# Hybrid decoder step: state updates in pairs, token rows at both ends, a split first unit and shorter last sums

## What is computed

```python
def _rmsnorm(x, g):
    y = x * rsqrt(mean(x * x, -1) + EPS)
    return y * g
def _swiglu(x, w_up, w_down):
    g, u = split(x @ w_up, 2)
    return (silu(g) * u) @ w_down
# every sublayer f:   x = x + (1/2 or 1) * _rmsnorm(f(_rmsnorm(x, pre)), post)
# mLSTM, state of a sample sequence and head after its four tokens:
C = carry_decay * C + einsum('bhl,bhld,bhle->bhde', w_state, k, v)   # 128 x 256 each
n = carry_decay * n + einsum('bhl,bhld->bhd', w_state, k)
```

## Time and profile before

| | us |
|---|---|
| median of 3 runs | 2698.49 (2693.58 to 2698.68) |
| the profiled execution | 2698.88 |
| its span in the profile | 2697.2 |
| TensorE busy | 2634.7 (98%) |
| VectorE busy | 1529.4 (57%) |
| ScalarE busy | 1161.6 (43%) |
| chain that ended last | TensorE 92%, VectorE 4%, ScalarE 2% |

### The profile page before, as it was taken

One profiled execution on the slowest core, in us unless ns is written; L12 is line 12 of the kernel. 1 busy time (PEld: TensorE's weight loads), 2 busy tenths in 40 slices (PEclk: granted clock), 3 DMA queues, 4 the chain that ended last, 5 costly groups with the idle time before them and its releaser, 6 DMA issues.

```text
span 2697.2 us, 51800 instructions
## 1 busy us (share of the span) xinstructions
PE 2634.7 (98%) x22023; PEld 2496.1 (93%) x22023; DVE 1529.4 (57%) x1891; ACT 1161.6 (43%) x1577; POOL 302.1 (11%) x305
## 2 busy tenths in 40 slices
PE   7999999999999999999999999999999999999998
PEld 6999987999999986699999999799999999989998
DVE  4556855655565545465555554465556558656654
ACT  4334644533444444353443443253344446444442
POOL 1000005100200045010010001010020000052000
PEclk9999999999999999899999999999999999999999
DMA  5445523454544645444455463354455455234543
GB/s 191 160 145 166 157 84 104 156 164 142 178 157 147 196 130 166 127 156 159 148 168 164 148 200 114 117 181 163 145 168 172 139 172 164 84 97 156 171 137 99
DMA packets 415625, 404.24 MB, mean 150 GB/s; under 512 B 14786, under 2 KB 411950, under 8 KB 415086
## 3 DMA queue, kind: packets, MB, share of 16 engines
q1 hardware_dynamic: 411348, 397.43, 46.6%
q0 software_dynamic: 4096, 4.20, 0.5%
HBM read 385.20 MB, written 16.39 MB: 149 GB/s over the span
## 4 chain that ended last, share of the span: by engine, by line
PE 92%; DVE 4%; ACT 2%; issue 1%; DMA 0%; SPq 0%; DVEq 0%; ACTq 0%
PE psum L379 22%; PE psum L380 22%; PE psum L381 22%; PE psum L541 2%; PE psum L545 2%; PE psum L542 2%; DVE w_lo L361 1%; PE psum L2792 1%; PE psum L1153 1%; PE psum L1170 1%; PE psum L2154 1%; PE psum L2805 1%; PE psum L1165 1%; ACT w_hi L344 1%; PE psum L1248 1%
## 5 line engine op out<-in xcount | busy, mean ns | idle before, releaser
L361 DVE TENSOR_TENSOR w_lo<-raw,w_hi 128x2048 fp32r<-128x2048 f32 (+2 forms) x362 | 745.0, 2058 | 515.6 <-ACT w_hi L344 515.4
L379 PE MATMUL psum<-xn_hi,w_hi 128*128 128x288 f32 x3232 | 963.0, 298 | 8.3 <-DVE w_lo L361 7.3
L380 PE MATMUL psum<-xn_lo,w_hi 128*128 128x288 f32 x3232 | 955.0, 295 | 0.0
L381 PE MATMUL psum<-xn_hi,w_lo 128*128 128x288 f32 x3232 | 951.7, 294 | 0.0
L344 ACT ACTIVATE w_hi<-raw 128x2048 fp32r<-128x2048 f32 (+2 forms) x350 | 598.7, 1710 | 800.9 <-PE psum L381 737.4
L379 PEld LDWEIGHTS psum<-xn_hi,w_hi 128*128 128x128 f32 x3232 | 607.1, 188 | 15.8 <-issue 5.9
L381 PEld LDWEIGHTS psum<-xn_hi,w_lo 128*128 128x128 f32 x3232 | 610.2, 189 | 0.0
L380 PEld LDWEIGHTS psum<-xn_lo,w_hi 128*128 128x128 f32 x3232 | 608.4, 188 | 0.6
L380 PE MATMUL psum<-h_lo,w_hi 128*128 128x288 f32 x1408 | 415.5, 295 | 0.0
L379 PE MATMUL psum<-h_hi,w_hi 128*128 128x288 f32 x1408 | 415.0, 295 | 0.0
L381 PE MATMUL psum<-h_hi,w_lo 128*128 128x288 f32 x1408 | 414.9, 295 | 0.0
(11 more groups left out here) (583 smaller groups left out, 3155.7 us busy)
## 6 DMA issues: line engine op xcount, KB each, us to landing
raw<-w_ffn_up SPq DMA_DIRECT2D x176, 1024.0 KB, 5.1
raw<-w_ffn_down SPq DMA_DIRECT2D x64, 768.0 KB, 4.4
raw<-w_ffn_down SPq DMA_DIRECT2D x64, 640.0 KB, 4.0
raw<-gdn_w_in SPq DMA_DIRECT2D x32, 1024.0 KB, 5.7
raw<-mlstm_w_in SPq DMA_DIRECT2D x12, 1024.0 KB, 5.4
raw<-gdn_w_out SPq DMA_DIRECT2D x8, 1024.0 KB, 5.6
raw<-cache_mla_latent SPq DMA_DIRECT2D x64, 128.0 KB, 2.5
a_split<-cache_mla_latent SPq DMA_DIRECT2D x64, 128.0 KB, 2.2
```

Of the source, the lines that this page charges most:

```text
L361: dve.tensor_tensor(spread(w_lo[slot(u, i)], u), packed(raw[u % NRAW], u), spread(w_hi[slot(u, i)], u).bitcast(F32), ALU.subtract).then_in ...
L379: pe.matmul(out, wh[:, k, c], hi(k), start=st, stop=False)
L380: pe.matmul(out, wh[:, k, c], lo(k), start=False, stop=False)
L381: last = pe.matmul(out, wl[:, k, c], hi(k), start=False, stop=sp_)
```

## The change

There are four edits in it. (1) The 32 state updates are made in 16 pairs, after chunks 1, 4, 7 (tiles 2 to 5), 2, 6 (tile 6) and 1, 5 (tile 7). A pair is two heads of one sequence, so two different quarters of rows; it waits until VectorE has read both results of the pair before. VectorE updates in the same order; SyncE stores heads in twos and loads the output units ahead of or behind these stores; the fill is 13 products and 4 of half width. (2) At the start the transposes go by token tiles, each as its tile lands; only the first 128 vectors (gains) are awaited, loaded on ScalarE's queue; the other vectors' transposes stand between units 0 and 1. Three products on ones run first. (3) Unit 0 comes in two transfers, is split in halves between the parts of x, and TensorE multiplies unit 0 alone, then unit 1. (4) For the last sublayer the sums over tokens use x's columns as the loaded operand and one moving column, so that token t's root stands in partition t. x and y are both turned to rows by halves of a token tile, ScalarE and VectorE keep x's rows, and VectorE adds y times the root in one operation; SyncE stores half rows. VectorE adds one of the last two squares to the total.

```diff
             if u >= NRAW:
                 sp.wait_ge(lo_ready, u - NRAW + 1)
+            if u == 0:
+                sp.dma_start(wview(raw[0], 0)[:, 0:H], units[0][0][:, 0:H]).then_inc(sem("first_in"), 16)
+                sp.dma_start(wview(raw[0], 0)[:, H:KC], units[0][0][:, H:KC]).then_inc(raw_in[0], 16)
+                return
...
         def pe_leave_part(pe, n):
 
+            if n == LAST:
+                return
...
+        def act_first(act):
...
+            act.wait_ge(sem("first_in"), 16)
+            part(w_hi[slot(0)], 0, first_half).then_inc(first_hi, 1)
+            act.wait_ge(vec_ready, 1)
+            act.wait_ge(x_loaded, 5)
+            for k in range(KC):
+                act.activation(xn_hi[:, k, :], x[:, k, :], ACT.Copy, scale=gain(l, g, k)).then_inc(xhi_ready, 1)
+                if k == H - 1:
+                    act.wait_ge(raw_in[0], 16)
+                    part(w_hi[slot(0)], 0, last_half).then_inc(hi_ready, 1)
+            act.wait_ge(raw_in[1], 16)
+            part(second_hi, 1, first_half).then_inc(first_hi, 1)
+            part(second_hi, 1, last_half).then_inc(second_hi_ready, 1)
+            act.activation(eps_t[:, 2:3], eps_t[:, 0:1], ACT.Copy).then_inc(hi_ready, 1)
+            for i in range(H):
+                act_square_x(act, 0, i)
+            act_split_half(act, ubase[0] + 2, 0)
+            act_split_half(act, ubase[0] + 2, 1)
+            act.wait_ge(vec_ready, 4)
+
+        def dve_first(dve):
...
+            dve.wait_ge(first_hi, 1)
+            part(w_lo[slot(0)], w_hi[slot(0)], 0, first_half).then_inc(first_lo, 1)
+            for k in range(KC):
+                dve_low_x(dve, 0, k)
+                if k == H - 1:
+                    dve.wait_ge(hi_ready, 1)
+                    part(w_lo[slot(0)], w_hi[slot(0)], 0, last_half).then_inc(lo_ready, 1)
...
+            if n == 0:
+                pe_enter_unit(pe, 0, [o for o in outs if o[0] == 0], (lo_ready, 1))
+                pe_vectors(pe)
+                pe_enter_unit(pe, 0, [o for o in outs if o[0] == 1], (second_lo_ready, 1))
+                pe.wait_ge(vec_ready, 2)
+                return
...
+                if n == LAST and k == 2 * H - 2:
+                    dve.wait_ge(sq_sum, summed(2 * LAST + 1))
+                    dve.tensor_tensor(sq_total, sq_total, sq[:, k, :], ALU.add).then_inc(sem("last_sum"), 1)
...
+        updated_state = lambda q: (2 * (q // (2 * NB)) + q % 2, q // 2 % NB)
...
-            for h in range(LH):
-                once(sp, "l_c_new", 8 * h + 8)
-                sp.dma_start(a["ml_C_s"][g, :, h].rearrange("b d e -> d b e"), Cin[h][:, :, 0:LC]
-                             ).then_inc(sem(("l_c0_saved", "l_c_out0")[h > 0]), 16)
-                sp_unit(sp, u0 + 13 + h)
+            sp_unit(sp, u0 + 13)
+            for p in range(2):
+                once(sp, "l_c_new", 16 * p + 16)
+                for h in (2 * p, 2 * p + 1):
+                    sp.dma_start(a["ml_C_s"][g, :, h].rearrange("b d e -> d b e"), Cin[h][:, :, 0:LC]
+                                 ).then_inc(sem(("l_c0_saved", "l_c_out0")[h > 0]), 16)
+                for u in ((u0 + 14, u0 + 15), (u0 + 16,))[p]:
+                    sp_unit(sp, u)
...
-            pe_filled(pe, u0 + 13, 2, 15)
+            pe_filled(pe, u0 + 13, 2, 13)
+            pe_filled(pe, u0 + 13, 2, 4, T // 2)
...
-                if k in ((0, 2, 3, 5, 7), (0, 1, 2, 4, 5, 6))[t > 5] and ups:
-                    ml_update(pe, ups.pop(0))
+                if k in ((1, 4, 7), (2, 6), (1, 5))[max(t - 5, 0)] and pairs:
+                    ml_update(pe, pairs.pop(0))
...
-        def ml_update(pe, q):
-
-            h, b = q // NB, q % NB
-            if q == 0:
+        def ml_update(pe, j):
+
+            if j == 0:
                 once(pe, "l_kd_s", 1)
                 once(pe, "l_vm", 1)
-            elif q == 1:
                 once(pe, "l_hs", 1)
             else:
-                once(pe, "l_c_new", q - 1)
-            pe.matmul(psum[:, 6 + q % 2, 0:LC + 1], LKDs[quarter(h), :], Vm[quarter(h), b, :], start=True, stop=True
-                      ).then_inc(sem("l_u"), 1)
+                once(pe, "l_c_new", 2 * j)
+            for q in (2 * j, 2 * j + 1):
+                h, b = updated_state(q)
+                pe.matmul(psum[:, 6 + q % 2, 0:LC + 1], LKDs[quarter(h), :], Vm[quarter(h), b, :], start=True, stop=True
+                          ).then_inc(sem("l_u"), 1)
...
-            updated(range(20, 26))
+            updated(range(24, 28))
             o_last(6)
-            for k in range(3):
-                updated(range(26 + k, 27 + k))
+            updated(range(28, 30))
+            for k in range(2):
                 gated(k)
-            updated(range(29, 32))
+            updated(range(30, 32))
+            gated(2)
             o_last(7)
...
+        def pe_load(pe):
+
+            pe.wait_ge(warm, 1)
+            for _ in range(3):
+                pe.matmul(psum[:, 7, 0:T], rr[:, 0, 0:P], rr[:, 0, :], start=True, stop=True)
+            pe.wait_ge(sem("base_in"), 16)
+            pe.wait_ge(sem("gains_in"), 16)
+            pe.transpose(psum[:, 5, 0:P], vt[:, 0, :], ident).then_inc(vec_turned, 1)
+            for t, (cols, _, _) in enumerate(token_tiles):
+                m = cols.stop - cols.start
+                pe.wait_ge(sem(f"x_in{t}"), 16)
...
+            pe.wait_ge(y_copied, H * LAST + 3)
+            pe.wait_ge(sem("last_sum"), 1)
+            sums(sq_total, True, False)
+            pe.wait_ge(sq_ready, last_squares + H + 1)
+            sums(sq[:, 2 * H - 1, :], False, True)
+            turn(x, 4, 0, 0, x_turned)
+            turn(y, y_rows[0][0], 0, 0, y_turned)
+            pe.wait_ge(y_copied, H * LAST + H)
+            turn(x, 6, 0, 1, x_turned)
+            turn(y, y_rows[0][1], 0, 1, y_turned)
+            for j in range(2, 6):
+                pe.wait_ge(*((x_kept_first, 1) if j == 2 else (x_kept, j - 2)))
+                turn(x, (4, 6)[j % 2], j // 2, j % 2, x_turned)
+                if j == 5:
+                    pe.wait_ge(r_ready, 2 * NSUB + 1)
+                turn(y, y_rows[j // 2][j % 2], j // 2, j % 2, y_turned)
...
             for t, (cols, src, _) in enumerate(token_tiles):
-                sp.dma_start(xin(t)[0:cols.stop - cols.start], src).then_inc(sem("x_in"), 16)
-            for dst, src in vec_rows:
+                sp.dma_start(xin(t)[0:cols.stop - cols.start], src).then_inc(sem(f"x_in{t}"), 16)
+            sp_unit(sp, 0)
+            sp_unit(sp, 1)
+            for dst, src in vec_rows[1:]:
                 sp.dma_start(dst, src).then_inc(sem("vec_in"), 16)
...
+                part = rows[0:m, t, 512 * h:512 * h + 512]
+                dve.scalar_tensor_tensor(out=part, in0=psum[0:m, y_rows[t][h], :], scalar=rcol[0:m, t:t + 1], in1=part,
+                                         op0=ALU.mult, op1=ALU.add).then_inc(row_done, 1)
```

More of the change, by code:

```diff
@@ L3146, in trunk @@
                 r += m
+        x_turned, vec_turned, warm = sem("x_turned"), sem("vec_turned"), sem("warm")
+        rows = at("rows", [P, 3, D], 2 * FC * T + 4 * T)
+        rcol = rr[:, 1, 0:4]
+        y_rows = ((0, 1), (2, 3), (7, 5))
+        y_turned, row_done, x_kept, x_kept_first = sem("y_turned"), sem("row_done"), sem("x_kept"), sem("x_kept_first")
+        last_squares = squares_before(2 * LAST + 1)
+        def pe_load(pe):
[8 more added lines that the diff above has]
+                pe.wait_ge(sem(f"x_in{t}"), 16)
+                for k in range(KC):
+                    out = psum[:, 2 * t + k // H, (k % H) * m:(k % H) * m + m] if t < 2 else psum[:, 4, k * m:(k + 1) * m]
+                    last = pe.transpose(out, xin(t)[0:m, k * P:(k + 1) * P], ident[0:m, 0:m])
+                    if k == KC - 1 or t < 2 and k == H - 1:
+                        last.then_inc(x_turned, 1)
+            pe.wait_ge(vec_ready, 1)
@@ new lines, in keep_x, with pe_rows, turn, sums @@
+        def keep_x(eng, copy, j, kept):
+            t, h = j // 2, j % 2
+            m = token_tiles[t][0].stop - token_tiles[t][0].start
+            eng.wait_ge(x_turned, 5 + j + 1)
+            copy(rows[0:m, t, 512 * h:512 * h + 512], psum[0:m, (4, 6)[j % 2], :]).then_inc(kept, 1)
+        def pe_rows(pe):
+            def turn(src, bank, t, h, done):
+                cols = token_tiles[t][0]
+                for q in range(H):
+                    last = pe.transpose(psum[0:cols.stop - cols.start, bank, q * P:(q + 1) * P], src[:, H * h + q, cols], ident)
+                last.then_inc(done, 1)
+            def sums(src, first, last):
+                for t, (cols, _, _) in enumerate(token_tiles):
+                    ins = pe.matmul(psum[0:cols.stop - cols.start, 5, t:t + 1], src[:, cols], ones[:, 0:1],
+                                    start=first and t == 0, stop=last, skip_group_check=True)
+                if last:
+                    ins.then_inc(ss_done, 1)
+            pe.wait_ge(y_copied, H * LAST + 3)
```

(1 more changed line is left out.)

178 lines of the change are left out of this document (104 added, 74 removed).

## The result

Of the changed kernel four runs gave a median of 2671.1 us (2667.96 to 2676.69) beside 2698.6 (2693.58 to 2701.68) for the kernel before: ratio 0.990, 95% interval 0.988 to 0.9925. Two later comparisons of the same file gave 2674.0 (ratio 0.9906) and 2672.7 (0.990). All 14 runs together have a median of 2672.1 and lie between 2665.98 and 2676.85. Forecast were 2672.8 and 2667 to 2681. The first profiled execution took 2670.29 us with a span of 2668.3 (before 2698.88 and 2697.2). One run of the kernel before, taken later, needed 4263.0 us at a mean granted clock of 0.555; it is left out of every comparison here.

What follows compares the result with a forecast made beforehand. TensorE, busy 98% of the span, was taken as the bound, so only its waits, low clock or avoidable work could pay: 9.7 + 9.9 + 6.1 = 25.7 us off 2698.5 gives 2672.8 us, range 2667 to 2681.

Steps and rivals of the forecast that it cites:

- Start: Kernel start: first product near 12.4, unit 2 at 27.7 instead of 37.5; gain 9.7 us, bounds 7.5 and 12.
- Rival (b): Start: three matmuls on a constant raise the clock, which stays up until 12.4; 2.4 us more, 2670.4; 12%.
- 25.3 given as the bound: Start: with the clock high from 12.4 on, VectorE's parts are the bound and unit 2 begins at 25.3.
- Rival (e): Start: first tokens or gains land late; it gains 7.5 at most or the first unit waits; 2675 to 2677; 11%.
- Tiles: mLSTM stage: 16 paired visits at 0.86 replace 32 single ones; 47.3 us, gain 9.9, bounds 10.6 and 4.0.
- its waits: mLSTM tiles: new TensorE waits at pairs 0 and 1, in tile 4 and in tile 7, together 2.55 us.
- Rival (a): mLSTM tiles: a pair's passes go in series, a visit costs 1.25 and the stage gains 4; 2678.7; 10%.
- SyncE: Behind the tiles: last output unit's load stands behind 2 MB of state writes, about 6 us; no cost.
- End: Last sublayer: sum L462 leaves (0.5 us), new order of sums and transposes; gain 6.1 us, bounds 4 and 6.6.
- Rival (c): End: half clock from about 2684, full tiles' turns cost 0.86, result 2 us later; 2674.8; 15%.
- Rival (d): mLSTM stage: clock granted at half for the 47.3 us, up to 47 us more; 2720; 2%.

Runs made afterwards that it cites:

- busy_until_entry: The changed kernel with eight more products on ones put into TensorE's gaps at the start: 2668.9 us, ratio 0.9899 to the kernel before.
- same_quarter: The changed kernel, but both updates of a pair belong to one head and use the same quarter of TensorE's rows: 2677.6 us, ratio 0.9922.

## Why the prediction was right, point by point

**Start, forecast 9.7, measured 8.8** (8.1 to 9.6 in the six profiles with this start). The order of steps held, the sizes moved. The second tile landed at 8.1, not 6.5; the short transposes stood behind it, and the first product came at 13.04 instead of 12.4. The low clock lasted 5.1 us of products, to 18.2, not 4.1. Together 1.1 us (0.6, and half of one more slow microsecond, 0.5), for the 1.0 between unit 2 at 28.7 and the 27.7 of the forecast. When the clock rises differs from profile to profile (17.2 to 19.1), and unit 2 with it, so a part of this is the execution and not the forecast. Rival (b), the warm start, did not happen in any of the six, and busy_until_entry and the two kernels that share its start show that filled gaps bring it about: their 25.6 to 26.2 stand beside the 25.3 given as the bound. Rival (e) came true in its first half: the second tile was late, but the start gained more than 7.5. Two small sums of the prediction are off without effect: 10.6 and 0.43 are 11.0, not 11.2, and 21.1 and 7 are 28.1, not 28.4.

**Tiles, forecast 47.3, measured 47.34 to 47.36** in eight profiles. A pair's visit costs 0.63 to the next product and, with the change of rows, 0.82 in all: the distance of two pairs with three chunks between them is 2.02 (1682.94 to 1684.96), three chunks are 1.20. The forecast had taken 0.86, which was 0.6 us too much over 16 visits; its waits were 0.2 too small (0.5, 0.45, 0.9, 0.7 against 0.47, 0.28, 1.31, 0.67), and the rest is 47.34 - 19.2 - 13.1 - 2.7 = 12.3 instead of 11.8. The three errors cancel, so the exact hit is partly luck. Rival (a) is out by the timeline (0.70), and same_quarter shows what it would have looked like.

**SyncE, forecast "No cost", measured 1.1 us** (0.9 to 1.0 in two more profiles of the file). This is the step that failed, the smallest in price. It asked only whether the last output unit comes in time, and it did. But with two heads of a sequence in a pair, heads 2 and 3 end together, 2 MB of states leave behind the last update, SyncE waits for these stores, and behind that wait stand the next layer's units. From output product to entry it is 31.8 us instead of 30.7, and storing the first half earlier brings it back to 30.6.

**End, forecast 6.1 with the 0.5 of L462, measured 6.0 to 6.6 without it** (the 0.5 itself lies between products and was not measured apart). Turns cost 0.44, not 0.48. The last VectorE operation ends 8.0 behind the last product's start, the 2.4 behind it measured 2.7. Rival (c), the end at half clock, is out: 1.00 in both windows, and between its turns TensorE nowhere stands still for a microsecond. The Trainium skill, "TensorE: Matmul & The Clock Gate", Part 4, had spoken for it, by what it states of transpose mode; whether these transposes are made in that mode no run here shows. Here 44 of the 48 took 4.97 us on the chain, 0.11 each, which is the high clock, and did not bring it down; at the start eight behind the products on ones took 1.10 us together. The measurement decides for this kernel. Rival (d) is out too: no window of the tiles has a clock under 1.00.

**Sum.** 8.8 + 10.05 - 1.1 + 0.2 (between tiles and output product, 2.22 instead of 2.41) + 6.0 to 6.6 + 0.5 = 24.4 to 25.0, forecast 25.7. The median of all runs of before (38 in five comparisons) is 2698.5, of the changed kernel 2672.1: 26.4. The 1.4 to 2.0 between the parts and the medians are open; they are well inside the intervals (0.988 to 0.9925 is 20 to 32 us). So that 2672.8 and 2672.1 agree this closely is partly luck; that the parts hold within 1.1 us each is not. The first profile alone (28.9) would have taught the wrong sizes.

## What to carry to other kernels

When an edit makes several results ready at the same moment, look at everything that queues behind their stores, up to the next stage's loads, and not only at the load that stands right beside them. A wait of TensorE behind a long operation of another engine can go by cutting that operation in two and placing the halves between the short ones. Before a difference in one profile is explained, take the same file's profile once more: stages of unchanged code had lengths 3 and 4 us apart here. And put the mean granted clock beside each run's time: 0.001 of it was worth 2 to 3 us.

## What the runs showed of the hardware

- Two products of 32 rows from different quarters cost TensorE no more than one (0.70 us for four passes and for two), from the same quarter 1.13. The Trainium skill, "TensorEngine Tiling (Array Packing)", Tiling Modes, says that row tiles work independently and that a change of mode drains the engine; the rows agree with the first and bear out a price for the second (0.39 for the change and back).
- A transfer of 0.5 MB issued at 1.8 landed after 4.7 us in the kernel before. It took 6.3 (5.8 to 6.9 in ten profiles) when 2 MB of weights were issued behind it by 3.8 us and the gains had gone ahead on a second queue, and 5.6 in the one profile that held the weights back. What part the weights have in it is not shown beyond that.
- VectorE's split of 2.28 us took 3.56 beside GpSimd's sums, and GpSimd's last sum 2.73 instead of 0.81 (rows of the changed kernel below). The Trainium skill, "SBUF — State Buffer", SBUF: two separate sides, says that an operation of VectorE with two SBUF inputs and a GpSimd operation that reads SBUF shut each other out; the direction agrees, and so does the size: GpSimd's operation before ended at 25.07, and 2.28 behind that is 27.35, where the split ended at 27.22. Here it cost nothing, as unit 2 was split by 27.2 and wanted at 28.7.

```profile
23.66 3.56 DVE L365 TENSOR_TENSOR w_lo<-raw,w_hi 128x2048 fp32r<-128x2048 f32 x1
25.15 2.73 POOL L440 TENSOR_TENSOR fbuf<-fbuf 128x288 f32<-128x288 f32 x1
```
